# A transformer kernel on one core: the second block's first layer starts with the keys and values of its context, and its input norm runs between them

## The chip, the cores and the metric

The program runs on one core of one Trainium2 chip. The metric is the device time of one execution in microseconds (us). TensorE (PE in the views) does the matrix products, VectorE (DVE), ScalarE (ACT) and GpSimd (POOL) do the elementwise work, SyncE (SP) issues nearly all transfers. Each engine runs its own list of instructions in order and waits on semaphores for the others.

## The reference

Two blocks of two layers work on 256 tokens of width 1024 in float32. The second block also has a context of 256 rows. What matters here is the seam: the first block ends with a norm, and the first layer of the second block opens with another norm and projects tokens and context with the same weights.

```python
return rmsnorm(h, final_norm)                      # end of the first block
...
h = _rms(x, norm_w) * (1.0 + sc[:, None, :]) + sh[:, None, :]      # tokens
hc = _rms(xc, norm_w) * (1.0 + sc_c) + sh_c                        # context
aq, ak, av, az, dq, dk, dv, dz, bf, bz, cu, cv, cz = _split_in(h @ w_in)
aqc, akc, avc, azc, dqc, dkc, dvc, dzc, bfc, bzc, cuc, cvc, czc = _split_in(hc @ w_in)
...
ka = jnp.concatenate([ka_c, _k_heads(ak, kn_a, A_KV_HEADS, tabs)], axis=1)
va = jnp.concatenate([va_c, _heads(av, A_KV_HEADS)], axis=1)
```

The context rows `hc` don't depend on the first block's output; only the tokens `h` do.

## The kernel before

Every weight matrix is cut into chunks of 128x2048 float32, and the list FLOW is their order of use. A chunk comes in as two halves. SP loads a half into one of four stage buffers (line 220) once the half four places earlier has been split. ACT copies it to WH, the high part (`high`, L227), and DVE writes the rest to WL, the low part (`low`, L232). WH and WL hold two chunks each, so ACT may start on a chunk only when PE is done with the one two places back. `high_next` and `low_next` stand in the programs of ACT and DVE at the places where the next chunk is split. A product of activations and weights is three matmuls (lines 299 to 301, or 296 to 298 where tokens are the rows of the result), since the activations are split as well, into XH and XL. Columns NOW (0 to 255) of XH, XL and X are the tokens, columns CTX (256 to 511) the context.

The seam between the blocks goes as follows on PE. The first block's last product writes the eighth piece of X. `final_tensor` then does two sums of squares over the tokens (L1682), two means (L1689, four matmuls with one column of result) and two inverses spread over all rows (L1696, four matmuls). Between these, `final_vector` and `final_gpsimd` turn the mean into an inverse root: four short DVE instructions (L1707 to L1714), a power on POOL (L1740), one short DVE instruction (L1716) and two copies (L1721). With the first inverse, `adapted_vector` and `adapted_scalar` make XH and XL of the tokens for eight values of k: a scaled copy on DVE (L410), the high part on ACT (L421), the low part on DVE (L405), named `n00.x0` to `n00.x7`. The context's XH and XL (`n01.x0` to `n01.x7`) are made during the last products of the first block. Then `keys_tensor` runs: queries of two branches (chunks 0 and 3 of `in_0`, four results of 128x512), keys (chunk 1, two results of 128x512, tokens and context in one matmul) and values (chunk 4, 2 results, 96 matmuls with 256 columns). Behind it stands `squares_tensor`, for the norms of queries and keys (L1845, L1849, then the rotary product L445). The raw queries and keys are copied and squared on ACT (L1903, L1905), the values copied on DVE (L1868). PSUM has eight banks that `tile` gives out in turn.

Of the kernel before, what the change touches and what calls it, by code (L numbers as in the profile page):

```python
# [113 lines left out]
def build(nc, A, out):  # L114
    ctx = ExitStack()
    with ctx:
# [73 lines left out]
                FLOW += [("nsa_gates", 0)] + [("nsa_in", c) for c in (4, 5, 6, 8, 7, 9, 0, 1, 2, 3)]  # L190
                FLOW += [("nsa_out", c) for c in range(4)]
        for l in range(2):
            FLOW += [(f"in_{l}", c) for c in (0, 3, 1, 4, 2, 5, 8, 9, 10, 7, 6)]
            FLOW += [(f"merge_{l}", c) for c in range(20)]
            FLOW += [(f"out_{l}", c) for c in range(4)]

# [1428 lines left out]
        def shift2(l, v):  # L1625
            return lambda k: MODS[l][:, k, v:v + 1]
# [49 lines left out]
        def final_tensor(e):  # L1676
            b = [tile(e, f"fn.sums{i}") for i in range(2)]
            for i in range(2):
                for k in range(8):
                    g = slice(32 * (k % 4), 32 * (k % 4) + 32)  # L1680
                    e.wait_ge(*ac.of(f"{('fn', 'n00')[i]}.sq{k}"))
                    t = e.matmul(b[i][g, 0:256], C("onerow", 0, 32), (SQ0, SQ1)[i][:, k, :], start=k < 4, stop=k >= 4)  # L1682
                t.then_inc(*pe.tick(f"fn.sums{i}"))
            b = tile(e, "fn.mean")
            e.wait_ge(*ve.of("fn.part0"))
            e.wait_ge(*ac.of("fn.part1"))
            for i in range(2):
                for n in range(2):
                    t = e.matmul(b[:, 2 * i + n:2 * i + n + 1], B.wide[i][:, n * 128:(n + 1) * 128], C("psum1"), start=True,  # L1689
                                 stop=True)  # L1690
            t.then_inc(*pe.tick("fn.mean"))
            for i in range(2):
                b = tile(e, f"fn.inv{i}")
                e.wait_ge(*ve.of(f"fn.wide{i}"))
                for n in range(2):
                    t = e.matmul(b[:, n * 128:(n + 1) * 128], B.wide[i][:, n * 128:(n + 1) * 128], ident, start=True,  # L1696
                                 stop=True)
                t.then_inc(*pe.tick(f"fn.inv{i}"))

        def final_vector(e):  # L1700
            e.tensor_tensor(B.gain, MODS[0][:, 8:16, 0], P("final_norm", 0, 8), ALU.mult).then_inc(*ve.tick("fn.gain"))
            e.wait_ge(*pe.of("fn.sums0"))
            e.tensor_copy(B.wide[0], banks["fn.sums0"][:, 0:256]).then_inc(*ve.tick("fn.part0"))
            banks.emptied("fn.sums0", ve)
            e.wait_ge(*pe.of("fn.mean"))
            b = banks["fn.mean"]
            e.tensor_scalar(B.m[:, 0:2], b[:, 0:2], EPS, None, ALU.add).then_inc(*ve.tick())  # L1707
            e.wait_ge(*ve.now())
            e.reciprocal(B.u, B.m[:, 0:2]).then_inc(*ve.tick())
            e.wait_ge(*ve.now())  # L1710
            e.tensor_tensor(B.u, B.u, b[:, 2:4], ALU.mult).then_inc(*ve.tick())
            banks.emptied("fn.mean", ve)
            e.wait_ge(*ve.now())
            e.tensor_scalar(B.m[:, 2:4], B.u, EPS, None, ALU.add).then_inc(*ve.tick("fn.mean"))  # L1714
            e.wait_ge(*gp.of("fn.pow"))
            e.tensor_tensor(B.r[:, 2:4], B.r[:, 2:4], B.r[:, 0:2], ALU.mult).then_inc(*ve.tick())  # L1716
            for i in range(2):
                r = B.r[:, 2 - 2 * i:4 - 2 * i].rearrange("p (a n) -> p a n", n=1).to_broadcast([128, 2, 128])
                if i == 0:
                    e.wait_ge(*ve.now())  # L1720
                e.tensor_copy(B.wide[i].rearrange("p (a n) -> p a n", a=2), r).then_inc(*ve.tick(f"fn.wide{i}"))  # L1721
            e.wait_ge(*pe.of("fn.inv0"))
            run(adapted_vector(e, "n00", X[:, :, NOW], lambda k: B.gain[:, k:k + 1], shift2(0, 0),
                               banks["fn.inv0"][:, 0:256], SQ0, NOW, "fn.inv0"))
            e.wait_ge(*pe.of("fn.inv1"))
            for k in range(8):
                e.scalar_tensor_tensor(out=X[:, k, NOW], in0=X[:, k, NOW], scalar=P("final_norm", k),
                                       in1=banks["fn.inv1"][:, 0:256], op0=ALU.mult, op1=ALU.mult).then_inc(*ve.tick("fn.x"))
            banks.emptied("fn.inv1", ve)

        def final_scalar(e):
            e.wait_ge(*pe.of("fn.sums1"))
            e.activation(B.wide[1], banks["fn.sums1"][:, 0:256], ACT.Copy).then_inc(*ac.tick("fn.part1"))
            banks.emptied("fn.sums1", ac)
            run(adapted_scalar(e, "n00", shift2(0, 0), SQ0, NOW))

        def final_gpsimd(e):
# [76 lines left out]


        def keys_tensor(e, flow, L):
            l, NT, nt = L.l, L.NT, L.nt
            for br, c in enumerate(QUERIES):
                w = Chunk(flow, f"in_{l}", c)
                for a in range(2):  # L1820
                    b = tile(e, f"k{l}{br}.q{a}")
                    x = (lambda k: e.wait_ge(*ve.of(f"n{l}0.x{k}"))) if br + a == 0 else None
                    features(e, b[:, 0:NT], w, a * 128, f"k{l}{br}.q{a}", x, L.xs())
                w.done()
            w = Chunk(flow, f"in_{l}", KEYS)
            for br in range(2):
                b = tile(e, f"k{l}{br}.k")
# [6 lines left out]
                for t in range(2):  # L1834
                    rows(e, b[:, t * 256:(t + 1) * 256], w, 2 * j + t, slice(0, 256), f"l{l}.v{j}")
            w.done()
            squares_tensor(e, L, 0)

        def squares_tensor(e, L, br):

# [20 lines left out]

        def keys_vector(e, flow, L):
            l = L.l
            for c in range(4):
                low_next(e, flow)
            for j in range(2):
                e.wait_ge(*pe.of(f"l{l}.v{j}"))
                e.tensor_copy(L.V[:, 2 * j:2 * j + 2, :, :], banks[f"l{l}.v{j}"].rearrange("p (t b c) -> p t b c", t=2, b=2)).then_inc(  # L1868
                    *ve.tick(f"l{l}.v"))
                banks.emptied(f"l{l}.v{j}", ve)  # L1870
            squares_vector(e, L, 0)

        def squares_vector(e, L, br):
# [23 lines left out]
        def keys_scalar(e, flow, L):  # L1897
            l, NT = L.l, L.NT
            def raw(br, a, name, n):
# [5 lines left out]
                e.activation(L.S3[br][:, a, 0:n], v, ACT.Square).then_inc(*ac.tick(f"{p}.sq"))  # L1905
                banks.emptied(f"{p}.{name}", ac)

            for br in range(2):
                high_next(e, flow)
                for a in range(2):  # L1910
                    raw(br, a, f"q{a}", NT)
            high_next(e, flow)
            for br in range(2):
                raw(br, 2, "k", 512)
            high_next(e, flow)

        def keys_gpsimd(e, L, br):
            p = f"k{L.l}{br}"
# [434 lines left out]
        def tensor(e):  # L2353
# [3 lines left out]
            ffn_tensor(e, flow, 0, iter(()))  # L2357
            nsa_tensor(e, flow, rings)
            ffn_tensor(e, flow, 1, context_tensor(e))
            final_tensor(e)  # L2360
            layer_tensor(e, flow, rings, LAYERS[0])
            meet(e, "l0.end")
            run(rms_tensor(e, "n10", SQM[0], lambda k: e.wait_ge(*ac.of(f"n10.sq{k}"))),
# [3 lines left out]
        def vector(e):  # L2367
# [2 lines left out]
            ffn_vector(e, flow, 0, "nn", iter(()))  # L2370
            nsa_vector(e, flow)
            ffn_vector(e, flow, 1, None, context_vector(e))
            final_vector(e)
            layer_vector(e, flow, LAYERS[0])
            meet(e, "l0.end")
            between_vector(e)
# [2 lines left out]
        def scalar(e):  # L2379
# [2 lines left out]
            ffn_scalar(e, flow, 0, "nn", iter(()))  # L2382
            nsa_scalar(e, flow)
            ffn_scalar(e, flow, 1, None, context_scalar(e))
            final_scalar(e)
            layer_scalar(e, flow, LAYERS[0])
            meet(e, "l0.end")
            for v in range(2):
# [246 lines left out]
```

## Time and profile before

| | |
|---|---|
| median of 3 runs | 1497.08 us (1496.42 to 1498.44) |
| profiled execution, its own time | 1496.34 us |
| its span in the profile | 1494.4 us |
| PE busy | 1434.9 us, 96% of the span |
| DVE busy | 781.1 us, 52% |
| ACT busy | 638.4 us, 43% |
| POOL busy | 176.7 us, 12% |

The span goes from the first to the last instruction that the profiler recorded. The profiled execution's own time is 1.94 us longer than its span. The profile says for each wait what released it, and for each stretch the granted clock of TensorE (PEclk), 1.00 at 2.4 GHz and 0.50 at 1.2 GHz.

### The profile page before, as it was taken

Reading aid. Unit: us, or ns where it says so; the run is one execution under the profiler, and the core shown is the slowest. Engines: PE = TensorE matmul, PEld = TensorE weight load, DVE = VectorE, ACT = ScalarE, POOL = GpSimd, SP = SyncE. Lnnn points to the kernel's source line nnn. Section 1 sums busy time; section 2 is a strip of 40 time slices with the busy share of each in tenths; the row PEclk is TensorE's granted clock in tenths of the full one; section 3 lists DMA queues with packets and bytes.
Section 4 is the critical chain, followed back from the end, with each engine's and each line's share of the span. In section 5 each row is a group of like instructions: output and inputs, shape, how many; then the busy total and the mean of one; then the engine's idle time right before and its main releaser. Section 6 shows DMA issues by size and latency. Waiting matters only on the chain.

```text
span 1494.4 us, 24718 instructions
## 1 busy us (share of the span) xinstructions
PE 1434.9 (96%) x10418; PEld 1278.5 (86%) x10418; DVE 781.1 (52%) x1207; ACT 638.4 (43%) x1105; POOL 176.7 (12%) x149
## 2 busy tenths in 40 slices
PE   9999999999899899999899999899999979998998
PEld 8989999999755699999888876788888869878998
DVE  6876555546546665654623356433233363574554
ACT  5645444443355554445432344433232243454452
POOL 0010211001200011110004000021111002201110
PEclk9999999999999999999999999999999989999999
DMA  8435655454487445554331310222223213314553
GB/s 309 139 122 178 212 184 181 172 184 145 167 287 265 154 170 191 177 188 151 113 114 57 102 57 1 83 86 98 100 85 112 86 53 116 132 57 141 177 191 113
DMA packets 56974, 211.16 MB, mean 141 GB/s; under 512 B 6176, under 2 KB 9888, under 8 KB 53536
## 3 DMA queue, kind: packets, MB, share of 16 engines
q1 hardware_dynamic: 56128, 206.40, 40.2%
q10 hardware_dynamic: 736, 3.18, 0.6%
q8 instruction: 83, 1.36, 0.4%
q14 instruction: 27, 0.22, 0.0%
HBM read 208.51 MB, written 1.05 MB: 140 GB/s over the span
## 4 chain that ended last, share of the span: by engine, by line
PE 89%; DVE 5%; ACT 3%; DMA 1%; POOL 1%; issue 1%; SPq 0%; ACTq 0%; POOLq 0%; DVEq 0%
PE psum L299 24%; PE psum L300 23%; PE psum L301 23%; PE psum L1153 2%; PE psum L1174 2%; DVE WL L232 2%; PE psum L1307 2%; PE psum L298 2%; PE psum L297 2%; PE psum L296 2%; PE psum L2177 1%; PE psum L1463 1%; PE psum L1157 1%; PE psum L445 1%; ACT WH L227 1%
## 5 line engine op out<-in xcount | busy, mean ns | idle before, releaser
L299 PE MATMUL psum<-XH,WH 128*128 128x256 f32 (+1 forms) x2048 | 638.1, 312 | 13.5 <-DVE WL L232 8.5
L300 PE MATMUL psum<-XL,WH 128*128 128x256 f32 (+1 forms) x2048 | 630.4, 308 | 0.0
L301 PE MATMUL psum<-XH,WL 128*128 128x256 f32 (+1 forms) x2048 | 629.6, 307 | 0.0
L232 DVE TENSOR_TENSOR WL<-stage,WH 128x1024 fp32r<-128x1024 f32 x334 | 397.9, 1232 | 319.7 <-ACT WH L227 319.5
L227 ACT ACTIVATE WH<-stage 128x1024 fp32r<-128x1024 f32 x334 | 335.1, 1051 | 363.6 <-PE psum L301 323.7
L299 PEld LDWEIGHTS psum<-XH,WH 128*128 128x128 f32 x2048 | 396.1, 193 | 41.5 <-issue 17.5
L300 PEld LDWEIGHTS psum<-XL,WH 128*128 128x128 f32 x2048 | 396.7, 194 | 16.8 <-issue 0.5
L301 PEld LDWEIGHTS psum<-XH,WL 128*128 128x128 f32 x2048 | 396.6, 194 | 16.8
L2333 POOL TENSOR_TENSOR arena<-arena,con 128x512 f32<-128x512 f32 (+1 forms) x48 | 51.4, 1070 | 400.3 <-DVE con L2264 399.7
L1265 ACT ACTIVATE arena<-psum,SM 128x16 f32<-128x16 f32 (+3 forms) x144 | 67.4, 478 | 25.9 <-DVE SM L1201 11.8
L1250 ACT ACTIVATE arena<-psum 128x512 f32<-128x512 f32 (+2 forms) x48 | 35.4, 737 | 79.8 <-PE psum L1174 79.6
L299 PE MATMUL psum<-hidden,WH 128*128 128x256 f32 x224 | 63.1, 282 | 5.1 <-DVE hidden L1033 5.1
L1113 POOL TENSOR_TENSOR arena<-arena,SM 128x512 f32<-128x512 f32 x22 | 42.7, 1939 | 196.3 <-ACT arena L1087 196.3
L301 PE MATMUL psum<-hidden,WL 128*128 128x256 f32 x224 | 63.1, 282 | 0.0
L300 PE MATMUL psum<-hidden,WH 128*128 128x256 f32 x224 | 62.4, 279 | 0.0
L2264 DVE TENSOR_TENSOR con<-psum,con 128x512 f32<-128x512 f32 (+1 forms) x48 | 26.3, 554 | 59.4 <-ACT con L2121 30.7
L2121 ACT ACTIVATE con<-psum,par 128x512 f32<-128x512 f32 (+1 forms) x64 | 35.6, 572 | 50.2 <-PE psum L301 50.2
L1196 DVE TENSOR_REDUCE SM<-psum 128x2 f32<-128x1024 f32 (+4 forms) x48 | 41.9, 873 | 28.7 <-PE psum L1157 15.9
L296 PE MATMUL psum<-WH,XH 128*128 128x256 f32 (+1 forms) x192 | 55.5, 289 | 0.0
L298 PE MATMUL psum<-WH,XL 128*128 128x256 f32 (+1 forms) x192 | 54.6, 284 | 0.0
L297 PE MATMUL psum<-WL,XH 128*128 128x256 f32 (+1 forms) x192 | 54.5, 284 | 0.0
L1153 PE MATMUL psum<-arena 64*128 64x256 f32 (+3 forms) x288 | 44.4, 415 | 5.5 <-POOL arena L466 4.0
(255 smaller groups left out, 1700.3 us busy)
## 6 DMA issues: line engine op xcount, KB each, us to landing
stage<-w SPq DMA_DIRECT2D x132, 512.0 KB, 4.5
stage<-merge SPq DMA_DIRECT2D x80, 512.0 KB, 4.6
ring<-ada SPq DMA_DIRECT2D x24, 1024.0 KB, 5.2
stage<-in SPq DMA_DIRECT2D x44, 512.0 KB, 4.7
stage<-ab_in SPq DMA_DIRECT2D x24, 512.0 KB, 4.9
stage<-nsa_in SPq DMA_DIRECT2D x20, 512.0 KB, 4.8
stage<-out SPq DMA_DIRECT2D x16, 512.0 KB, 4.6
stage<-ab_out SPq DMA_DIRECT2D x8, 512.0 KB, 4.2
```

The lines of the kernel that those rows point to most:

```text
L227: e.activation(hi, raw, ACT.Copy).then_inc(s_hi, 1)
L232: e.tensor_tensor(lo, raw, hi.bitcast(F32), ALU.subtract).then_inc(s_lo, 1)
L296: e.matmul(dst, xh, wh, start=start, stop=False)
L297: e.matmul(dst, xh, wl, start=False, stop=False)
L298: return e.matmul(dst, xl, wh, start=False, stop=stop)
L299: e.matmul(dst, wh, xh, start=start, stop=False)
L300: e.matmul(dst, wh, xl, start=False, stop=False)
L301: return e.matmul(dst, wl, xh, start=False, stop=stop)
L1113: e.tensor_tensor(F.sg[c % 3], F.sg[c % 3], spread(RT, 2, 256), ALU.mult).then_inc(*gp.tick(f"{p}.gate{c}"))
L1153: t = e.matmul(v[:, q, h, :], query(h)[r], key[r], start=h == 0 or u.mask is None, stop=u.mask is None)
L1265: e.activation(s[:, q, h, :], v[:, q, h, :], ACT.Exp, bias=nm[:, q, h:h + 1], scale=rate, accum_out=sm[:, q, h:h + 1]).then_inc(*ac.tick(f ...
L2333: e.tensor_tensor(L.M[:, m, :], L.M[:, m, :], L.T2[n % 2], ALU.add).then_inc(*gp.tick(f"u{l}.{n}"))
```

## The change

In layer 0 of the second block the chunks of `in_0` are used in the order keys, values, queries, queries. PE does the sums of the seam's norm first, then products of the context that need none of its results: the context's half of both key results, with the means and the inverses put between them, and the context's values. After that come the token half of the keys, the values of the tokens and both queries. `final_tensor` becomes a generator, stepped by `context_keys_tensor`. On DVE and ACT the splitting of the value chunk moves into `final_vector` and `final_scalar`. Layer 1 keeps its order, except that DVE copies its two value results in the opposite order.

```diff
-            FLOW += [(f"in_{l}", c) for c in (0, 3, 1, 4, 2, 5, 8, 9, 10, 7, 6)]
+            FLOW += [(f"in_{l}", c) for c in ((1, 4, 0, 3), (0, 3, 1, 4))[l] + (2, 5, 8, 9, 10, 7, 6)]
...
                 t.then_inc(*pe.tick(f"fn.sums{i}"))
+            yield
             b = tile(e, "fn.mean")
...
             t.then_inc(*pe.tick("fn.mean"))
+            yield
             for i in range(2):
                 b = tile(e, f"fn.inv{i}")
...
             e.tensor_scalar(B.m[:, 2:4], B.u, EPS, None, ALU.add).then_inc(*ve.tick("fn.mean"))
+            low_next(e, flow)
             e.wait_ge(*gp.of("fn.pow"))
...
             banks.emptied("fn.sums1", ac)
+            high_next(e, flow)
             run(adapted_scalar(e, "n00", shift2(0, 0), SQ0, NOW))
...
         def keys_tensor(e, flow, L):
+            if L.l == 0:
+                context_keys_tensor(e, flow, L, final_tensor(e))
+                queries_tensor(e, flow, L)
+            else:
+                queries_tensor(e, flow, L)
+                all_keys_tensor(e, flow, L)
+            squares_tensor(e, L, 0)
...
+        def context_keys_tensor(e, flow, L, norm):
+
+            l = L.l
+            wk, wv = Chunk(flow, f"in_{l}", KEYS), Chunk(flow, f"in_{l}", VALUES)
+            next(norm)
+            keys = [tile(e, f"k{l}{br}.k") for br in range(2)]
+
+            def between(br, k):
+                if br == 0:
+                    e.wait_ge(*ve.of(f"n{l}1.x{k}"))
+                if k == 4:
+                    next(norm)
+
+            for br in range(2):
+                features(e, keys[br][:, CTX], wk, br * 128, f"k{l}{br}.ck", lambda k: between(br, k), CTX)
+
+            def values(j):
+                b = tile(e, f"l{l}.v{j}")
+                for t in range(2):
+                    rows(e, b[:, t * 256:(t + 1) * 256], wv, 2 * j + t, slice(0, 256), f"l{l}.v{j}")
+
+            values(1)
+            for k in range(8):
+                e.wait_ge(*ve.of(f"n{l}0.x{k}"))
+                for br in range(2):
+                    t = product(e, keys[br][:, NOW], wk, k, slice(br * 128, br * 128 + 128), XH[:, k, NOW], XL[:, k, NOW],
+                                k == 0, k == 7)
+                    if k == 7:
+                        t.then_inc(*pe.tick(f"k{l}{br}.k"))
+            wk.done()
+            values(0)
+            wv.done()
...
-            for c in range(4):
+            for c in range(l * 4):
                 low_next(e, flow)
-            for j in range(2):
+            for j in (1, 0):
+                if l == 0:
+                    low_next(e, flow)
                 e.wait_ge(*pe.of(f"l{l}.v{j}"))
...
+            if l == 0:
+                for br in range(2):
+                    raw(br, 2, "k", 512)
+                high_next(e, flow)
             for br in range(2):
                 high_next(e, flow)
```

On PE, at the seam, the order before is this, with the query products behind the three steps of the norm:

```order
L301 MATMUL psum<-hidden,WL 128x256
L1682 MATMUL psum<-arena,con 32x256 x16
L1689 MATMUL psum<-con,SM 128x1 x4
L1696 MATMUL psum<-con,SM 128x128 x4
L299 MATMUL psum<-XH,WH 128x512
```

With the change the means stand behind 12 context products with 256 columns (three per value of k, the last three are shown), and in the same way the inverses, now L1698, behind 24 more:

```order
L299 MATMUL psum<-XH,WH 128x256
L300 MATMUL psum<-XL,WH 128x256
L301 MATMUL psum<-XH,WL 128x256
L1690 MATMUL psum<-con,SM 128x1 x4
L299 MATMUL psum<-XH,WH 128x256
```

In place of 48 key matmuls with 512 columns PE has 96 with 256, and nothing else is added to its list.

On DVE the four short instructions, the wait for POOL and the copies follow each other before:

```order
L1709 RECIPROCAL SM<-SM 128x2
L1711 TENSOR_TENSOR SM<-SM,psum 128x2
L1714 TENSOR_SCALAR SM<-SM 128x2
L1716 TENSOR_TENSOR SM<-SM 128x2
L1721 COPY SM<-SM 128x256 x2
L410 SCALAR_TENSOR_TENSOR arena<-X,SM,psum 128x256 x2
```

With the change the two low halves of the value chunk (L232) stand inside this chain, ahead of the instruction that waits for POOL (L1720):

```order
L1712 RECIPROCAL SM<-SM 128x2
L1714 TENSOR_TENSOR SM<-SM,psum 128x2
L1717 TENSOR_SCALAR SM<-SM 128x2
L232 TENSOR_TENSOR WL<-stage,WH 128x1024 x2
L1720 TENSOR_TENSOR SM<-SM 128x2
L1725 COPY SM<-SM 128x256 x2
```

On ACT the raw keys come first, and the two query chunks are split right behind them (x4), where before a chunk's two halves stood between the copies:

```order
L1737 ACTIVATE SM<-psum 128x256
L227 ACTIVATE WH<-stage 128x1024 x2
L421 ACTIVATE XH<-arena,MOD 128x256 x8
L1956 ACTIVATE arena<-psum,par 128x512
L1958 ACTIVATE arena<-psum 128x512
L1956 ACTIVATE arena<-psum,par 128x512
L1958 ACTIVATE arena<-psum 128x512
L227 ACTIVATE WH<-stage 128x1024 x4
```

The high halves of the value chunk have moved ahead of the eight high parts of the tokens.

## Rows read from the trace of the kernel before

**Rows 1.** The page: shares of the chain that ended last, by engine.

```profile
PE 89%; DVE 5%; ACT 3%; DMA 1%; POOL 1%; issue 1%; SPq 0%; ACTq 0%; POOLq 0%; DVEq 0%
```

**Rows 2.** PE in order of time at the seam: start us, us, instruction, idle before.

```profile
729.63 2.52 PE L1682 MATMUL psum<-arena,con 128*32 128x256 f32 x32
732.72 1.02 PE L1689 MATMUL psum<-con,SM 128*128 128x1 f32 x8 [0.56 <-ACT SM L1733]
736.28 2.04 PE L1696 MATMUL psum<-con,SM 128*128 128x128 f32 x8 [2.55 <-DVE SM L1721]
739.16 0.76 PE L299 MATMUL psum<-XH,WH 128*128 128x512 f32 x1 [0.83 <-DVE XL L405]
```

**Rows 3.** Stretches: length, busy by engine (count), PEclk, DMA share, GB/s.

```profile
732.70:736.10 3.40, 1.02 (x8) 0.95 (x8) 1.07 (x7) 0.00 (x0) 1.01 (x1) 1.00 0.00 0
736.10:742.90 6.80, 5.79 (x17) 4.78 (x18) 5.44 (x15) 3.21 (x7) 0.00 (x0) 0.50 0.00 0
787.30:794.10 6.80, 6.80 (x18) 4.92 (x18) 3.88 (x6) 0.12 (x1) 5.04 (x4) 0.50 0.03 10
```

**Rows 4.** The chain that ended last, from 715 us: start us, us, what.

```profile
741.63 0.43 PE psum L301
...
785.32 0.79 PE psum L1845 x8
```

**Rows 5.** The same norm steps between full products elsewhere, on PE.

```profile
335.46 0.50 PE L340 MATMUL psum<-con,SM 128*128 128x1 f32 x4
335.82 0.36 PE L299 MATMUL psum<-XH,WH 128*128 128x256 f32 x1
...
338.77 0.61 PE L346 MATMUL psum<-con,SM 128*128 128x128 f32 x4
339.13 0.36 PE L299 MATMUL psum<-XH,WH 128*128 128x256 f32 x1
```

**Rows 6.** DVE in order of time at the seam and behind it.

```profile
734.36 0.17 DVE L1714 TENSOR_SCALAR SM<-SM 128x2 f32<-128x2 f32 x1
735.65 0.16 DVE L1716 TENSOR_TENSOR SM<-SM 128x2 f32<-128x2 f32 x1 [1.12 <-POOL SM L1740]
735.85 0.49 DVE L1721 COPY SM<-SM 128x256 f32<-128x256 f32 x2
737.51 0.87 DVE L410 SCALAR_TENSOR_TENSOR arena<-X,SM,psum 128x256 f32<-128x256 f32 x2 [1.17 <-PE psum L1696]
...
743.96 0.49 DVE L405 SCALAR_TENSOR_TENSOR XL<-arena,MOD,XH 128x256 fp32r<-128x256 f32 x1 [0.18 <-ACT XH L421]
...
747.57 2.36 DVE L232 TENSOR_TENSOR WL<-stage,WH 128x1024 fp32r<-128x1024 f32 x2
```

**Rows 7.** DVE and POOL at once, later: low halves beside POOL's additions; POOL's power.

```profile
791.50 3.43 DVE L232 TENSOR_TENSOR WL<-stage,WH 128x1024 fp32r<-128x1024 f32 x2
...
791.64 2.21 POOL L466 TENSOR_TENSOR arena<-arena 128x512 f32<-128x512 f32 x1
...
734.61 1.01 POOL L1740 TENSOR_TENSOR SM<-SM,con 128x4 f32<-128x4 f32 x1 [40.90 <-DVE SM L1714]
```

**Rows 8.** ACT at the seam and in the keys, and DVE's value copies.

```profile
732.19 0.38 ACT L1733 ACTIVATE SM<-psum 128x256 f32<-128x256 f32 x1 [1.17 <-PE psum L1682]
...
743.84 1.99 ACT L227 ACTIVATE WH<-stage 128x1024 fp32r<-128x1024 f32 x2
...
768.41 0.69 ACT L1903 ACTIVATE arena<-psum,par 128x512 f32<-128x512 f32 x1 [2.37 <-PE psum L301]
...
773.85 0.69 ACT L1903 ACTIVATE arena<-psum,par 128x512 f32<-128x512 f32 x1 [4.26 <-PE psum L301]
774.44 0.59 ACT L1905 ACTIVATE arena<-psum 128x512 f32<-128x512 f32 x1
...
779.61 0.69 DVE L1868 COPY arena<-psum 128x512 f32<-128x512 f32 x1 [1.24 <-PE psum L298]
785.36 0.69 DVE L1868 COPY arena<-psum 128x512 f32<-128x512 f32 x1 [5.07 <-PE psum L298]
```

More of the change, by code:

```diff
@@ L1698, in final_tensor, with final_vector @@
                 t.then_inc(*pe.tick(f"fn.inv{i}"))
-        def final_vector(e):
+            yield
+        def final_vector(e, flow):
             e.tensor_tensor(B.gain, MODS[0][:, 8:16, 0], P("final_norm", 0, 8), ALU.mult).then_inc(*ve.tick("fn.gain"))
@@ L1729, in final_vector, with final_scalar @@
             banks.emptied("fn.inv1", ve)
-        def final_scalar(e):
+        def final_scalar(e, flow):
             e.wait_ge(*pe.of("fn.sums1"))
@@ L1816, in keys_tensor, with queries_tensor @@
         def keys_tensor(e, flow, L):
-            l, NT, nt = L.l, L.NT, L.nt
+            if L.l == 0:
[5 more added lines that the diff above has]
+            squares_tensor(e, L, 0)
+        def queries_tensor(e, flow, L):
+            l, NT = L.l, L.NT
             for br, c in enumerate(QUERIES):
@@ L1824, in keys_tensor, with all_keys_tensor @@
                 w.done()
+        def all_keys_tensor(e, flow, L):
+            l = L.l
             w = Chunk(flow, f"in_{l}", KEYS)
@@ L1836, in keys_tensor @@
             w.done()
-            squares_tensor(e, L, 0)
+        def context_keys_tensor(e, flow, L, norm):
+            l = L.l
+            wk, wv = Chunk(flow, f"in_{l}", KEYS), Chunk(flow, f"in_{l}", VALUES)
[23 more added lines that the diff above has]
+            wv.done()
         def squares_tensor(e, L, br):
@@ L1870, in keys_vector @@
                 banks.emptied(f"l{l}.v{j}", ve)
+            if l == 0:
+                low_next(e, flow)
             squares_vector(e, L, 0)
@@ L1906, in raw @@
                 banks.emptied(f"{p}.{name}", ac)
+            if l == 0:
+                for br in range(2):
+                    raw(br, 2, "k", 512)
+                high_next(e, flow)
             for br in range(2):
@@ L1911, in keys_scalar @@
                     raw(br, a, f"q{a}", NT)
[L1912 to L1915, printed above, removed]
+            if l == 1:
+                high_next(e, flow)
+                for br in range(2):
+                    raw(br, 2, "k", 512)
+                high_next(e, flow)
         def keys_gpsimd(e, L, br):
@@ L2359, in tensor @@
             ffn_tensor(e, flow, 1, context_tensor(e))
-            final_tensor(e)
             layer_tensor(e, flow, rings, LAYERS[0])
@@ L2372, in vector @@
             ffn_vector(e, flow, 1, None, context_vector(e))
-            final_vector(e)
+            final_vector(e, flow)
             layer_vector(e, flow, LAYERS[0])
@@ L2384, in scalar @@
             ffn_scalar(e, flow, 1, None, context_scalar(e))
-            final_scalar(e)
+            final_scalar(e, flow)
             layer_scalar(e, flow, LAYERS[0])
```

## The prediction

> **What bounds the kernel now.** I read the chain that ended last first. PE makes up 89% of it and no other engine more than 5% [rows 1], so time is saved where PE waits or runs slowly, and a microsecond taken off there is taken off the end. Next comes PE in order of time at the seam between the blocks. The sums end at about 732.15 us (729.63 plus 2.52). Then PE waits three times, 0.56 us for the part copied by ACT, 2.55 us for the two copies on DVE and 0.83 us for the first piece of the tokens [rows 2]. For the whole span, 729.6 to 739.2 us hold only small instructions. The stretches show a second cost. In 732.70 to 736.10 PE was busy 1.02 of 3.40 us, and from 736.10 to 742.90 the granted clock was 0.50, that is 1.2 GHz [rows 3]. So the first queries ran at 0.43 us a matmul [rows 4], where a query tile of 24 such matmuls takes 5.44 us later (773.85 minus 768.41, the ACT copies of two results in turn [rows 8]), 0.227 us each. Last, the order before ends at 785.32 us, where `squares_tensor` starts [rows 4]. From there on both kernels give PE the same list, so the sum is that of PE's time from 732.15 to this point.
>
> **The change part by part.** Prices first. A product matmul with 256 columns: the two value results were copied at 779.61 and 785.36 [rows 8], 5.75 us for 48 matmuls, 0.120 us each. One with 512 columns: 0.227 us. The key products cost 96 times 0.120, 11.5 us, where 48 times 0.227, 10.9 us, stood: the split costs 0.6 us. Queries and values keep their prices, 21.8 us (four times 5.44) and 11.5 us.
>
> The means: at the seam four matmuls take 1.02 us alone [rows 2]. Between full products two of them take 0.36 us (335.46 to 335.82) and the inverse of one norm also 0.36 us (338.77 to 339.13) [rows 5]. The seam has twice as many of each, so 0.72 us for the means and 0.72 us for the inverses.
>
> Now in order. Twelve context products follow the sums: 732.15 plus 1.4 is 733.6 us. The part on ACT is ready at 732.57 (732.19 plus 0.38 [rows 8]), so the first wait is gone. The context's XH and XL were made during the last products of the first block. The means end at 734.3 us. Then 24 products, 2.9 us, to 737.2 us.
>
> Meanwhile DVE does its four short instructions. Before, PE's means ended at 733.74 and the fourth ended at 734.53 (734.36 plus 0.17 [rows 6]), 0.8 us later, so now at 735.1 us. Here stand the two low halves of the value chunk, 2.36 us [rows 6], whose high halves ACT made from 732.6 to 734.6 (1.99 us for two [rows 8]). They need the chunk in its stage buffers; the seam before moved nearly no data (DMA share 0.00 in both stretches [rows 3]), so it had landed. POOL's power, 1.01 us [rows 7], is released at the same moment. Do they run beside each other? The only rows that show low halves beside POOL are at 791.5 us: two of them took 3.43 us, 1.07 more than the 2.36 us elsewhere, beside an addition on POOL of 2.21 us [rows 7]. The low halves take two tensors from SBUF, as do the power and that addition (their forms say so), so I assume that they take turns. The price is between 0 (the power runs beside them) and 1.07 us, and I take 1.0, since this is the nearest row and the power is that long. Then DVE is through at 735.1 plus 2.36 plus 1.0, 738.5 us. From there it goes as before: from 735.65 to 736.28 us, start of the short instruction to start of the inverses, is 0.6 us [rows 6, 2]. The inverses start at 739.1 us, and PE has waited 1.9 us for them (0.9 if the price is 0).
>
> The Trainium skill (SBUF — State Buffer, Who interferes with whom) says that a DVE instruction with two SBUF inputs and a GpSimd instruction that reads SBUF exclude each other, and that the later one blocks for the whole of the other. The rows agree in their 1.07 us. By that rule the seam has one turn of waiting, by a rule of free overlap none: saved would be 5.1 us by the one and 6.1 us by the other.
>
> The inverses end at 739.8 us, the last 12 context keys at 741.3, the context's values (48 matmuls) at 747.0 us. The tokens: before, the first scaled copy started at 737.51 and the eighth low part ended at 744.45 us [rows 6], 6.9 us. Now they start with the first inverse at 739.5 and end at 746.4 us. The token keys start at 747.0, so all waits for tokens are hidden, and the cover is 0.6 us for the eighth piece, which is needed 5 us later still. If the inverses come 2 us late, PE comes late too, so the cover stays. Token keys end at 752.7 us, token values at 758.5, queries (21.8) at 780.2 us.
>
> The first query chunk is the next that could be late. ACT can split it only once the key chunk is used up (752.7) and after the raw keys, two results of 1.06 us each (0.59 to the square, 0.47 for it, from 773.85 and 774.44 [rows 8]), so at 755.0 us its first high half starts, at 756.0 DVE's low half, done at 757.2 us. PE asks for it at 758.5 us. The cover is the token values, 5.75 us, with 1.3 us to spare. Each microsecond beyond that would be on the path. The later chunks have more. DVE's last work on X ends 2 us later than before, in front of these halves, and POOL has nothing there. Behind 780.2 us DVE no longer has the value copy of 0.69 us and ACT has a raw query in its place, both beside PE's squares. In layer 1 the first value copy waits for the later result; it moves by 0.69 us beside PE's squares, and I price it at nothing. If that cover failed, it would cost at most these 0.69 us.
>
> The clock: before, it was 0.50 for 6.80 us at the seam. In the new order PE has full products around every small step, and its longest wait is 1.9 us in place of a stretch that holds 1.02 us of work in 3.40. I take the clock as held at 2.4 GHz. If it falls, half of a stretch at 1.2 GHz is lost, for 3.4 us of it 1.7 us and for 6.8 us 3.4 us.
>
> **The sum.** PE reaches the squares at 780.2 in place of 785.32 us: 5.1 us. It is made of 2.0 us of waits (3.9 before, 1.9 now), 1.8 us of slow queries (nine matmuls, 0.2 us too long each), 1.3 us of the inverses (2.04 before, 0.72 now), 0.3 us of the means and 0.3 us of rounding, less the 0.6 us of the split. Against the profiled execution's 1496.34 us that is 1491.2 us. The median of the runs shown is 0.74 us higher, so my time is 1492.0 us.
>
> **The rivals.**
> 1. The low halves don't hold up the power. PE waits only 0.9 us and the time is 1491.0 us. For it speaks that the power handles four elements per partition; against it the 1.07 us. Chance 0.15.
> 2. The clock falls at the inverses. The wait of 1.9 us and 0.7 us of small matmuls lie together. Price 1.7 to 3.4 us, time 1493.7 to 1495.4 us. For it speaks that the clock fell before at the seam, and at 787.3 us with PE counted as busy, while the norm's small matmuls ran [rows 3, 4]; against it the full products right before and behind. Chance 0.18.
> 3. The squares behind the queries keep the full clock. Before, they and the products behind them had 6.80 us at 0.50 [rows 3], which cost 3.4 us. They now start at another moment after another kind of product, so this may be lost or kept: 1488.6 us if it is gone. Chance 0.13.
> 4. The first query chunk comes late, because ACT does the raw keys first. From 1.3 us on it adds: 1 to 2 us late gives 1493 to 1494 us. Chance 0.05.
> 5. Slower: the clock stays low from the inverses through the context values and token keys. Their matmuls then take twice as long. At 1.2 GHz for 10.2 us the gain is eaten (5.1 us lost), and it decides from 16.4 us on, that is through to the queries: then 8.2 us are lost and the time is 1500.2 us. Against it: 6.80 us was the time at 0.50 before, with worse pauses. Chance 0.04.
>
> **How the numbers follow.** The forecast has 0.45. The range leaves out the slow end of the second rival, the fifth and the last tenths of the third: 1488.3 to 1495.0 us. Within 0.2% (3.0 us, about what a measurement of this kernel can tell from no change) is 1494.1 to 1500.1 us. Faster is all of the forecast, the first, third and fourth rivals and half of the second, with a little taken off for what I haven't seen: 0.83. The same 0.12, slower 0.05.
>
> **What would show it.** In the profile of the changed kernel: one wait of PE at the inverses of about 1.9 us, and none at the means or at the token keys; DVE's two low halves between the short instructions, together about 3.4 us long or the power late; granted clock 1.00 from the sums to the squares; the squares 5.1 us earlier than at 785.32. The prediction is wrong if PE waits for the first query chunk, if the clock falls in the context products, or if the stretch behind the squares takes another time than before.

## The result, and the profile after

| | before | with the change |
|---|---|---|
| median | 1498.44 us (5 runs, 1496.42 to 1499.23) | 1491.60 us (5 runs, 1490.61 to 1492.13) |
| ratio to before | | 0.9960, interval 0.9947 to 0.9972 |
| profiled execution, span | 1494.4 us | 1488.8 us |
| PE busy | 1434.9 us | 1431.9 us |

The change makes the kernel 4.2 to 7.9 us faster. The forecast was 1492.0 us. The median of before, from five runs, lies 1.36 us above that of the three shown earlier. So the median fell by 6.8 us, more than the 5.1 us of my sum, though the time itself came out 0.4 us from the forecast.

The chain of the changed kernel that ended last, from the sums on (start us, us, what). These are the lines that answer to [rows 4]:

```profile
732.36 2.45 PE psum L1682 x32
734.81 0.32 PE psum L299
...
736.42 0.80 PE psum L1690 x8
737.25 0.17 DVE SM L1710
...
738.00 2.26 DVE WL L232 x2
740.37 0.30 DVE SM L1725
740.67 0.14 issue
740.81 1.13 PE psum L1698 x8
741.93 0.12 PE psum L299
...
782.45 0.79 PE psum L1894 x8
```

The sums start at 732.36 us, and before at 729.70; nothing is changed ahead of them, so these 2.66 us are another matter (last section). From the sums to the squares it takes 50.1 us (782.45 minus 732.36) where it took 55.6 (785.32 minus 729.70). The seam has become 5.5 us shorter. I call this stretch the seam from here on.

All of PE's waits in it, and DVE and POOL in order of time, in the changed kernel:

```profile
PE psum L1698 <- DVE SM L1725: 0.6, 1, 0.6
```

```profile
737.83 0.17 DVE L1717 TENSOR_SCALAR SM<-SM 128x2 f32<-128x2 f32 x1
737.91 2.35 DVE L232 TENSOR_TENSOR WL<-stage,WH 128x1024 fp32r<-128x1024 f32 x2
740.18 0.15 DVE L1720 TENSOR_TENSOR SM<-SM 128x2 f32<-128x2 f32 x1
...
741.53 0.87 DVE L410 SCALAR_TENSOR_TENSOR arena<-X,SM,psum 128x256 f32<-128x256 f32 x2 [0.67 <-PE psum L1698]
...
747.98 0.49 DVE L405 SCALAR_TENSOR_TENSOR XL<-arena,MOD,XH 128x256 fp32r<-128x256 f32 x1 [0.18 <-ACT XH L421]
```

```profile
738.08 1.91 POOL L1745 TENSOR_TENSOR SM<-SM,con 128x4 f32<-128x4 f32 x1 [41.71 <-DVE SM L1717]
```

In place of three waits, 3.9 us in all [rows 2], there is one of 0.6 us. The low halves took 2.35 us, as if POOL were not there, and POOL's power took 1.91 us in place of 1.01 [rows 7]. It ended at 739.99 us, before the second low half (740.26), so that cost nothing. The tokens' last piece is ready at 748.47 us, and no wait for it is in the list. Stretches of the changed kernel (columns as in [rows 3]), up to the squares, to the second squares, and behind:

```profile
732.40:782.40 50.00, 49.37 (x338) 44.02 (x338) 22.86 (x46) 18.63 (x29) 1.91 (x1) 1.00 0.29 95
782.40:797.40 15.00, 15.00 (x80) 12.55 (x78) 5.86 (x7) 3.68 (x6) 10.04 (x6) 1.00 0.20 70
797.40:817.40 20.00, 20.00 (x100) 17.01 (x100) 5.51 (x9) 5.65 (x8) 8.31 (x6) 0.91 0.15 53
```

The granted clock is 1.00 through the seam, where it was 0.50 for 6.80 us [rows 3]. Behind the seam it is 1.00 up to the second squares (15 us, where the profile of the kernel before has 18.1) and 0.91 after them.

### The profile page after: what moved, and what is told of

Its sections match the earlier page's. It is cut to its first block, busy times and chain, and to the rows that moved or that the text cites. A ratio compares the mean times of both kernels' runs of the same rounds, so it can differ in the third digit from the quotient of the medians.

```text
span 1488.8 us, 24815 instructions
## 1 busy us (share of the span) xinstructions
PE 1431.9 (96%) x10466; PEld 1277.9 (86%) x10466; DVE 780.9 (52%) x1207; ACT 638.7 (43%) x1105; POOL 177.7 (12%) x149
## 3 DMA queue, kind: packets, MB, share of 16 engines
q8 instruction: 83, 1.36, 0.4%
## 4 chain that ended last, share of the span: by engine, by line
PE 90%; DVE 5%; ACT 2%; POOL 1%; issue 1%; DMA 0%; SPq 0%; ACTq 0%; POOLq 0%; DVEq 0%
PE psum L299 24%; PE psum L300 23%; PE psum L301 23%; PE psum L1153 2%; PE psum L1174 2%; DVE WL L232 2%; PE psum L1307 2%; PE psum L297 2%; PE psum L298 2%; PE psum L296 2%; PE psum L2235 1%; PE psum L1463 1%; PE psum L1157 1%; PE psum L445 1%; ACT WH L227 1%
## 5 line engine op out<-in xcount | busy, mean ns | idle before, releaser
L232 DVE TENSOR_TENSOR WL<-stage,WH 128x1024 fp32r<-128x1024 f32 x334 | 397.6, 1232 | 312.8 <-ACT WH L227 312.7
L299 PEld LDWEIGHTS psum<-XH,WH 128*128 128x128 f32 x2064 | 398.5, 193 | 40.6 <-issue 18.1
```

Of the source, the lines that this page charges most:

```text
L232: e.tensor_tensor(lo, raw, hi.bitcast(F32), ALU.subtract).then_inc(s_lo, 1)
L299: e.matmul(dst, wh, xh, start=start, stop=False)
```

## The experiments

Every kernel was profiled once, so each row below has one seam. "Squares" is the time from the first squares (L1845 in the kernel before) to the second, "clock" is the granted clock in the seam. The ratio is to executions of the kernel before made alongside (their medians are 1498.01 to 1498.44 us), with its interval; a dash means that only one execution was made.

| kernel | seam us | clock | squares us | median us | ratio |
|---|---|---|---|---|---|
| before | 55.6 | 0.94 | 18.1 | 1498.44 | |
| before again | 55.7 | 0.94 | 16.6 | 1498.82 | - |
| changed | 50.1 | 1.00 | 14.9 | 1491.60 | 0.9960 (0.9947 to 0.9972) |
| changed again | 50.1 | 1.00 | 16.5 | 1491.36 | 0.9957 (0.9945 to 0.9969) |
| norm's steps together, new order | 55.0 | 0.94 | 14.9 | 1493.68 | 0.9978 (0.9968 to 0.9987) |
| low halves behind the copies | 49.2 | 1.00 | 16.5 | 1489.02 | 0.9952 (0.9934 to 0.9969) |
| inverses 12 products later | 49.2 | 1.00 | 14.9 | 1489.06 | 0.9949 (0.9931 to 0.9968) |
| waits filled in the kernel before | 54.0 | 1.00 | 16.5 | 1492.60 | 0.9967 (0.9955 to 0.9979) |
| key products split in the kernel before | 56.2 | 0.94 | 14.9 | 1494.23 | - |
| queries last, nothing between | 57.9 | 0.91 | 16.5 | 1498.19 | 1.0003 (0.9994 to 1.0012) |
| first squares between products | see below | 1.00 | | 1488.96 | 0.9944 (0.9932 to 0.9957) |
| both squares between products | see below | 1.00 | | 1489.17 | 0.9940 (0.9927 to 0.9952) |
| inverses 21 products earlier | 54.8 | 0.94 | 16.5 | 1496.77 | 0.9993 (0.9984 to 1.0002) |

**The norm's steps together.** My theory was that the gain needs the norm's steps between products. The rival was that it is enough to have work in front that needs no tokens. From the changed kernel (on DVE the low halves also move behind the wide copies, as in the next kernel):

```diff
             wk, wv = Chunk(flow, f"in_{l}", KEYS), Chunk(flow, f"in_{l}", VALUES)
-            next(norm)
+            for _ in norm:
+                pass
...
-                if k == 4:
-                    next(norm)
```

> The new order of chunks, but all three steps of the norm stand together on PE ahead of the context products, as before the change; the value chunk's low halves on DVE stand behind the two wide copies. My theory (the gain needs the norm's steps between full products, for the waits and for the clock): PE waits about 0.6 us for the means and 2.6 us for the inverses again, the clock is at 1.2 GHz for some of the context products, and only the 0.8 us wait for the tokens is gone, less the 0.6 us of the split key products. From the first sum to the squares it takes 54 to 56 us (55.6 before, 50.1 with the change), and the time is within 2 us of the kernel before, about 5 us above the changed one. Rival (it is the order alone, the work that needs no tokens in front, that counts): 50 to 52 us from sums to squares, time within 2 us of the changed kernel.

The seam took 55.0 us, inside the 54 to 56 of my theory. PE's waits in this kernel:

```profile
PE psum L1698 <- DVE SM L1724: 2.5, 1, 2.5
PE psum L1690 <- ACT SM L1737: 0.6, 1, 0.6
```

The wait for the tokens is gone, the two others and the low clock (0.94 over the seam) are as before. So work in front that needs no tokens, by itself, brings 0.6 us at the seam. The expected time was wrong: the median is 4.6 us under that of the kernel before and 2.1 above the changed one's, nearly where the rival had it. The fall that isn't in the seam goes with a higher clock elsewhere (see "Medians and seams" below).

**The remaining wait.** Two kernels tried to remove the 0.6 us wait at the inverses, one by moving the low halves, one by moving the inverses:

```diff
-            low_next(e, flow)
             e.wait_ge(*gp.of("fn.pow"))
...
                 e.tensor_copy(B.wide[i].rearrange("p (a n) -> p a n", a=2), r).then_inc(*ve.tick(f"fn.wide{i}"))
+            low_next(e, flow)
```

> The changed kernel with the value chunk's two low halves on DVE behind the two wide copies in place of in front of POOL's power's result. Theory that the low halves set the remaining wait of PE at the inverses (0.63 us): the power takes 1.0 us again instead of 1.9, the wait at the inverses is gone, the seam from sums to squares takes 49.5 us in place of 50.1 us, the token pieces come at the same time or 0.3 us later, still in time. The time is 0.6 us below the changed kernel's, which is less than the runs can tell. Rival (the low halves cost nothing where they are, and moved they delay the tokens): seam 50.1 us or more, with PE waiting at the token keys.

```diff
-                if k == 4:
+                if br == 0 and k == 4:
                     next(norm)
...
             for br in range(2):
                 features(e, keys[br][:, CTX], wk, br * 128, f"k{l}{br}.ck", lambda k: between(br, k), CTX)
+            next(norm)
```

> The changed kernel with the inverses on PE behind all of the context's keys, 12 products later. Theory that PE's wait there is only a matter of lateness: the 0.63 us wait is gone, the tokens start about 0.8 us later (inverses start 1.4 us later less 0.6), still before the token keys, and the seam takes 49.5 us. Rival (the token pieces become late): PE waits at the token keys, up to 1 us, and the seam takes 50 to 51 us.

In both PE has no wait in the seam, and both seams took 49.2 us. In the first one POOL's power is short again:

```profile
736.26 1.01 POOL L1745 TENSOR_TENSOR SM<-SM,con 128x4 f32<-128x4 f32 x1 [41.71 <-DVE SM L1717]
```

In every profile with the low halves beside the power it takes 1.91 or 1.92 us (six), in every other 1.01. So they are what makes it longer, and they were the only thing that PE still waited for. Neither rival came: the tokens stayed in time with both. In the first of the two, ahead of PE's inverses DVE has now the copies alone, and the low halves fill the time in which DVE waited for the first inverse. The first scaled copy starts 9.6 us behind the start of the sums in place of 9.2, still in time. The medians are 2.3 to 2.6 us under the changed kernel's, more than the 0.9 us of the seam; the intervals overlap, so the rest isn't shown.

**The clock by itself.** The kernel before, with products that nobody reads in PE's waits:

```diff
+            def fill(n):
+                for i in range(n):
+                    e.matmul(fill_b[:, 0:256], fill_hi[:, i % 4, 0:128], XH[:, i % 4, CTX], start=True, stop=True)
...
+            fill(5)
             b = tile(e, "fn.mean")
...
             t.then_inc(*pe.tick("fn.mean"))
+            fill(21)
             for i in range(2):
...
                 t.then_inc(*pe.tick(f"fn.inv{i}"))
+            fill(10)
```

> The kernel before, with extra products in PE's waits at the seam: 5 behind the sums, 21 behind the means and 10 behind each inverse, 128 by 256 columns, of the context's high part and the first query chunk's high part, into a PSUM bank that nobody reads (their result is thrown away). Theory that more than half of the gain at the seam is the clock: it stays at 2.4 GHz, the inverses and first queries run at full speed, the waits themselves stay, and sums to squares takes 53 to 54 us in place of 55.6 us; the time is 2 us below the kernel before. The squares may keep or lose the clock as before. Rival (the clock fell too late to matter and the gain was waits alone): sums to squares 55.6 us or more, time that of the kernel before or slower by the extra products.

The text on record says ten behind each inverse; the kernel has ten behind the two together. The chain of this kernel at the seam:

```profile
732.97 0.67 PE psum L1698 x6
733.64 2.62 PE psum L1681 x21
736.26 1.06 PE psum L1706 x8
737.32 1.18 PE psum L1681 x10
738.55 0.47 PE psum L299
739.02 0.23 PE psum L300
```

L1681 is the filling, L1698 the means, L1706 the inverses. The inverses start 6.7 us behind the start of the sums, 6.6 before, so the fillings neither bring them forward nor hold them up, and the first queries run at 0.23 us a matmul in place of 0.43 [rows 4]. The seam took 54.0 us, in the expected 53 to 54: with the waits filled by useless work, the clock alone is worth 1.6 us here, net of what the filling added. The theory's wording, more than half of the gain at the seam, isn't borne out: 1.6 of 5.5 us is under a third. At full clock the first queries soon waited for the tokens' pieces (0.32 us for each first matmul of a piece, about 0.09 more than the others), which the slow clock had hidden. So 1.6 us is what this kernel shows, and a clock that holds without such waits can be worth more.

The median missed: 2 us under the kernel before were expected, and it is 5.7 under (3.1 to 6.7 by the interval). The filling isn't all that changed. From the second squares to the sums of the next layer's norm (L334) this kernel took 403.4 us, the kernel before 404.5 with the clock at 1.00 in both behind the second squares, and a wait of PE of 0.8 us for ACT there is missing. The extra `tile` moves all later results by one bank; that this is why was not tried.

**The price of the split.** The kernel before with 96 key matmuls of 256 columns in layer 0:

```diff
-                features(e, b, w, br * 128, f"k{l}{br}.k", x, slice(0, 512))
+                if l == 0:
+                    features(e, b[:, CTX], w, br * 128, f"k{l}{br}.ck", x, CTX)
+                    features(e, b[:, NOW], w, br * 128, f"k{l}{br}.k", None, NOW)
```

> The kernel before with the keys of layer 0 made in two halves of 256 columns each (context, then tokens), 96 matmuls in place of 48, nothing else. My term of the sum: 0.6 us more from sums to squares, 56.2 us in place of 55.6. Rival (the split is bound by the weight loads or by the bank switch): 58 us or more. The stretch from the first squares to the second squares was 18.1 us before and 14.9 us in the changed kernel; if the values in front of the squares are what lets the clock fall there, it is 16.5 to 18.1 us here as well.

56.2 us: the term of 0.6 us stands. The squares took 14.9 us here although the values stand in front of them, so the values there are not what lets the clock fall.

**The order alone.** Chunks in the new order, nothing between the norm's steps, keys with 512 columns (the low halves on DVE again behind the wide copies):

```diff
+            for _ in norm:
+                pass
+            w = Chunk(flow, f"in_{l}", KEYS)
+            for br in range(2):
+                b = tile(e, f"k{l}{br}.k")
+                x = (lambda k: (e.wait_ge(*ve.of(f"n{l}1.x{k}")), e.wait_ge(*ve.of(f"n{l}0.x{k}")))) if br == 0 else None
+                features(e, b, w, br * 128, f"k{l}{br}.k", x, slice(0, 512))
+            w.done()
```

> The chunks in the new order (keys, values, queries) but nothing put between the norm's steps and no split: norm, keys of tokens and context with 512 columns, values, queries. Seam as in the kernel before, sums to squares 55 to 56 us. Theory that the order also helps behind the seam (queries in front of the squares keep the clock at 2.4 GHz there, values in front of them don't): squares to second squares 14.9 us and a median about 3 us under the kernel before. Rival (what happens at the squares is chance, since it differs from one execution to the next): the stretch can be anything from 14.9 to 18.1 us and the median is within 1.5 us of the kernel before.

The seam took 57.9 us, a miss. PE's longest waits in this kernel were:

```profile
PE psum L1698 <- DVE SM L1724: 2.5, 1, 2.5
PE psum L299 <- DVE XL L405: 2.0, 1, 2.0
```

The wait for the first token piece is 2.0 us where it was 0.83 [rows 2]. I had left the value chunk's low halves, 2.35 us on DVE, behind the wide copies and ahead of the tokens. With no context products to cover them, they delay the tokens. The seam's clock fell to 0.91 on average. The median is that of the kernel before. So the new order of chunks brought nothing in this form; what it is worth with the low halves elsewhere was not run. The context products are also the cover of the moved low halves. That queries in front of the squares keep the clock there is refuted: 16.5 us here, and 14.9 us in the split with values in front.

**The inverses too early.** The changed kernel with three products between means and inverses in place of 24:

```diff
-                if k == 4:
+                if br == 0 and k in (4, 5):
                     next(norm)
```

> The changed kernel with the inverses on PE only three products behind the means in place of 24. PE then waits about 3.1 us for them in place of 0.6 (0.6 plus 21 products of 0.12 us). Theory that products between the steps hide the wait one for one, and the clock falls if they are missing: sums to squares 52.5 us if the clock holds, 54 to 55 us if it falls for one stretch. Rival (the clock holds at such a wait and all the gain is in other places): 52.5 us exactly, with the clock at 1.00 to the squares.

PE's waits and two stretches of it:

```profile
PE psum L1698 <- DVE SM L1725: 3.1, 1, 3.1
```

```profile
728.00:740.00 12.00, 9.28 (x89) 7.53 (x87) 6.16 (x14) 3.48 (x6) 1.91 (x1) 0.94 0.27 94
740.00:748.00 8.00, 7.59 (x45) 7.62 (x46) 6.54 (x17) 3.91 (x8) 0.00 (x0) 0.67 0.39 129
```

The wait is 3.1 us, as worked out, and the clock falls. The seam took 54.8 us: 50.1 plus 2.5 of waiting, and the other 2.2 came with the clock. This is the second rival of the prediction, forced. Its median is 1496.77 us, and its interval takes in no change. So the place of one call among the products decides over nearly the whole gain.

**The squares.** Their small matmuls put between the products of the last query tile, on top of the later inverses:

```diff
+                    if (l, br, a) == (0, 1, 1):
+                        steps = squares_steps(e, L, 0)
+                        x = lambda k: next(steps, None) if k > 0 else None
                     features(e, b[:, 0:NT], w, a * 128, f"k{l}{br}.q{a}", x, L.xs())
```

> The changed kernel with the inverses later (as in the earlier run) and with the small matmuls of the first squares put between the products of the last query tile, two at a time, the rotary product behind them. Theory that small matmuls cost most when they stand together (they take longer and the clock can fall): the sum of seam and squares, from the sums to the second squares, is 1 to 2 us shorter than the 64.1 us of the run with the later inverses, and the median 1 to 3 us under it. Rival (they already overlap as far as they can and the clock is no issue there): within 0.5 us of 64.1 us.

From the sums to the second squares it took 64.2 us (796.15 minus 731.92), where the later inverses alone have 64.1 (49.2 plus 14.9): the rival was right. The chain shows why:

```profile
776.38 0.34 PE psum L1906 x4
776.72 0.34 PE psum L299
...
782.11 0.34 PE psum L1912 x4
782.45 0.34 PE psum L299
783.25 1.29 PE psum L445 x4
...
796.15 0.79 PE psum L1906 x8
796.93 1.79 PE psum L1912 x16
```

Each pair of small matmuls takes 0.34 us, and the product behind it 0.34 in place of 0.23. So a pair costs 0.45 us there, 2.7 us for the six, and together they took 2.58 us, 0.43 a pair (0.79 plus 1.79 in the second squares of this kernel). The second squares too were then put between products, those of the second outer chunk:

```diff
+                    if l == 0 and c == OUTER[1][0] and a == 0:
+                        steps = squares_steps(e, L, 1)
+                        features(e, b[:, 0:NT], w, a * 128, f"l{l}.o{r}{a}", lambda k: next(steps, None) if k > 0 else None, L.xs())
```

> The changed kernel with the inverses later, with the small matmuls of both squares of layer 0 put between products. From the last profile: put between, the small matmuls cost as much as together, so what can still be won is the clock. Theory: no stretch at 1.2 GHz from the sums to the end of layer 0, where the changed kernel had one of 3.4 us behind the seam, and from the sums to the norm of the next layer 468.8 us or less, in place of 471.2; the median is 1487 to 1489 us. Rival (the clock falls somewhere else, or the attention starts late because its keys' norm comes later): 470 us or more, median 1490 us or more.

```profile
730.20:774.60 44.40, 44.40 (x317) 40.04 (x317) 22.86 (x46) 17.96 (x28) 1.92 (x1) 1.00 0.28 92
774.60:795.00 20.40, 20.40 (x101) 16.94 (x100) 4.79 (x7) 4.80 (x8) 9.90 (x6) 1.00 0.25 85
795.00:815.00 20.00, 20.00 (x108) 16.91 (x107) 7.75 (x11) 6.40 (x8) 8.30 (x6) 1.00 0.19 64
```

PE had no wait up to the end of these stretches, and the clock stayed at 1.00. From the sums to those of the next layer's norm it took 468.8 us, as expected. But the kernel with only the first squares put between has all this as well: clock 1.00 in the same three stretches, and 468.7 us. Every other profile has a clock of 0.81 to 0.91 between the first squares and 20 us behind the second ones. So the second edit has no effect that shows, and that the first one keeps the clock rests on these two profiles. The profiled span, 1484.8 us, is the shortest of all, but the median, 1489.17 us, is that of the kernels without this edit, just outside the 1487 to 1489 expected. The four variants with no wait at the inverses have medians of 1488.96 to 1489.17 us, some 2 us under the 1491.36 and 1491.60 us of the changed kernel, with intervals that overlap its own. They are the fastest kernels here, and the runs don't say which of the four is best.

**The two kernels once more.**

> The kernel before once more, for a second profile of it. If the clock at the squares is chance, the stretch from squares to second squares may be 14.9, 16.5 or 18.1 us; if it belongs to this kernel, 18.1 us again. From sums to squares 55.6 us within 0.5 us either way.

> The changed kernel once more, on the chip of the other two. Seam as in its first profile, 50.0 us from sums to squares, if its 0.6 us wait and full clock there are its own; 51.7 us or more with a stretch at 1.2 GHz if they were luck. Median 1491 to 1492.5 us.

Neither has an edit. Both seams repeated within 0.1 us (55.7 and 50.1 us), the wait of 0.6 us and the clock as well. What differs is behind them. The squares and the 20 us behind the second ones, in the first and second profile of the kernel before:

```profile
785.30:803.50 18.20, 18.20 (x80) 14.72 (x78) 6.18 (x8) 2.60 (x4) 10.01 (x6) 0.81 0.18 59
803.50:823.50 20.00, 20.00 (x107) 17.01 (x107) 7.13 (x11) 6.86 (x8) 8.47 (x6) 1.00 0.17 58
```

```profile
789.00:805.60 16.60, 16.60 (x80) 13.35 (x78) 6.21 (x8) 2.60 (x3) 9.94 (x6) 0.90 0.20 64
805.60:825.60 20.00, 20.00 (x101) 16.85 (x100) 5.37 (x9) 5.47 (x7) 8.57 (x6) 0.91 0.16 53
```

The changed kernel's second profile:

```profile
732.00:782.00 50.00, 49.37 (x337) 44.01 (x337) 22.85 (x46) 18.62 (x29) 1.91 (x1) 1.00 0.28 95
782.00:798.50 16.50, 16.50 (x77) 13.45 (x76) 6.05 (x7) 3.66 (x5) 9.90 (x6) 0.90 0.19 64
798.50:818.50 20.00, 20.00 (x101) 16.99 (x100) 5.57 (x9) 5.41 (x7) 8.28 (x6) 0.91 0.16 53
```

The changed kernel has the squares once in 14.9 us at clock 1.00 and once in 16.5 at 0.90. The column "squares us" alone misleads, for what is gained there can be lost behind. A longer stretch is safer, from the seam's sums to those of the next layer's norm: 478.2 and 478.4 us before, 471.1 and 472.7 with the change. Without the seam that is 422.6 and 422.7 before, 421.0 and 422.6 with the change. So one profile of the changed kernel gained 1.6 us behind the seam and the other nothing.

**Medians and seams.** In each kernel with several executions the median, against that of the kernel before, is lower than its seam accounts for, by 0.6 us (inverses early) to 4.0 us (norm's steps together, waits filled). The mean granted clock of every execution is on record, and it shows what goes with this. Its median is 0.982 for the kernel before, 0.986 and 0.984 for the changed one, 0.982 with the queries last, 0.983 with the inverses early, 0.9855 with the norm's steps together and 0.9875 with the waits filled. As an estimate, one minus this clock, times the span, is the time given up to the slow clock: 27 us before, 22 us with the norm's steps together. That kernel has the seam's low clock as before, so these 5 us are elsewhere. Its profile has 0.93 from 1200 to 1250 us, at the norm of the next layer, where the two of the kernel before have 0.86 and 0.90. Nothing is edited there, and why the clock fell less isn't shown.

## Why the prediction was right

It was right in sign and size, and at the seam also in place. In part the size is luck: the forecast of 1492.0 us hangs on the median of three executions, and from the median of five the same 5.1 us would give 1493.3. By its steps, each with the 2.66 us by which this execution came later to the sums:

- The first 12 products end and the means start at 736.42 us (forecast 736.3). The means end at 737.2 (forecast 737.0). The wait for ACT's part is gone.
- The wait at the inverses is the term that was mis-sized: 1.9 us forecast, 0.6 measured. The failing step was the price of the low halves beside POOL's power. I took 1.0 us from the pair at 791.5 us, where DVE's low halves had been held up. Here DVE lost nothing and POOL paid, 0.9 us, behind a cover. So the first rival, which I had given 0.15, was nearer with its wait of 0.9 us, but not in its reason: the low halves did hold up the power.
- Against that, the inverses took 1.13 us where I had 0.72. My price came from inverses of another norm between products, and even without a wait in front (the two kernels that removed it) they took 0.89 us here. The two errors leave 0.9 us, and the means and products took some 0.5 us more than I had: squares at 782.45 us, forecast 782.9.
- The split cost 0.6 us, measured by itself.
- All waits for tokens, value chunk and first query chunk were hidden, as worked out. ACT's high halves of the first queries started at 756.68 us, DVE ended with them at 760.15, and PE did not wait.
- The clock held. With the early inverses, a wait of 3.1 us came with 2.2 us of clock on top.
- The value copies of layer 1 cost nothing: from the first squares of that layer to the end of the span it is 234.8 us in both kernels.
- One of my own signs of being wrong came: the stretch behind the squares was to take the same time as before, and in the first profiles it took 14.9 us in place of 18.1. That is the third rival in part (chance 0.13, all of 3.4 us gone). Of the 3.2 us 1.7 were lost again behind the second squares, and in the second profiles the two kernels are alike there (16.6 and 16.5 us). So the forecast was met without it, but "the same list, the same time" doesn't hold between two executions.

Of the 5.5 us at the seam 3.3 are waits (3.9 to 0.6). The split takes 0.6 back, so 2.8 us are left for the slow queries, the inverses and the means, for which the sum had 3.4 us. The filled waits show 1.6 us of it alone, net of what they added; the rest is by subtraction.

The median fell by 6.8 us, the seam by 5.5. The rest of 1.3 us is within what differs between executions of one kernel (of it the first profile shows 1.6 us behind the seam and the second 0.1), and no run here shows that it belongs to the change.

## What to carry to other kernels

- At a chain of small dependent steps, look for large work that needs none of their results and put the steps between it, with as much work between two steps as the other engines need. Three products in place of 24 gave nearly the whole gain back.
- A chunk's preparation that is moved along needs its own cover. The same low halves were free beside context products and cost over a microsecond where these were missing.
- Compare the stretch that was edited, not only the whole. Here it repeats within 0.1 us, while executions of one kernel differ by 1.5 to 8 us. Take the stretch long enough to hold what may only move: the squares alone seemed to gain 3.2 us, and half of it was lost right behind.

## What was not expected of the hardware

- The granted clock falls in some executions of a kernel and not in others, at places that no edit touched. The kernel before reached the sums at 729.7 us in one profile and 733.4 in the other. Its squares took 18.1 and 16.6 us, the changed kernel's 14.9 and 16.5. In the clock this is 0.81, 0.90 or 1.00 over the stretch. What decides it stays open; from the sums to the next layer's norm, less the seam, it is worth 1.6 us in the two profiles of the changed kernel and 0.1 us in those of the kernel before.
- POOL's power of four columns takes 1.01 us alone and 1.91 us when it starts 0.17 us behind the first of two DVE instructions that take two tensors from SBUF. The second DVE instruction was not held up (2.35 us for both). By the Trainium skill (SBUF — State Buffer, Who interferes with whom) the later of the two blocks. The power did, and the second DVE instruction did not, though it started while the power had not ended: each half takes 1.2 us, so it started at about 739.1 us, and the power ended at 739.99. With the inverses later the trace gives the start itself, 739.54 us, and the power ended at 740.49. At the pair that I had priced from, both paid: DVE 1.07 us, and POOL's addition took 2.21 us [rows 7] where it took 1.29 at 810.78 us with DVE idle. So the power lost as much as that addition, 0.9 us, but did not hold DVE up in turn.
- Small float32 matmuls with two columns cost about the same between large products as in a row, 0.45 and 0.43 us a pair, so they do not hide in them.
